# The first feed-forward product of a two-block layer by Strassen's seven products, and the last second product in token halves

## The chip, the core and the metric

The kernel runs on one core of one Trainium2 chip. The metric is device time in microseconds (us), the median of three runs. TensorE (PE in the views) multiplies, VectorE (DVE) and ScalarE (ACT) do the elementwise work, SyncE (SP) issues the loads and stores.

## The reference, cut to what matters

Two transformer blocks over 512 tokens of width 1024, in float32. The change is in the end of the second block:

```
def squared_relu_mlp(u, w_ff1, w_ff2):            # w_ff1 1024x4096, w_ff2 4096x1024
    hdn = jnp.square(jax.nn.relu(jnp.einsum('bld,df->blf', u, w_ff1)))
    return jnp.einsum('blf,fd->bld', hdn, w_ff2)
h = h + squared_relu_mlp(rmsnorm_2(h, norm_ffn[l]), w_ff1[l], w_ff2[l])
return rmsnorm_2(h, norm_final)[:, N_META:]
```

## The kernel before

Activations lie transposed: X is eight tiles of 128 features by 512 tokens. Each float32 operand of a product is split into a rounded part (`_hi`, made by ScalarE) and the rest (`_lo`, a subtraction on VectorE). `mm3` (lines 545 to 547) issues three matmuls for one product of tiles: hi by hi, lo of the activations by hi of the weights, hi by lo. Every matmul has its own weight load.

Weights come in units of 1 MB (1024 x 256 values, "a unit"). SyncE loads a unit into one of two `raw` buffers as soon as VectorE has split the unit before the last (`w_lo_ready`). ScalarE writes `w_hi` (L1372, L1792), VectorE `w_lo` (L1813), each 128x2048 in one instruction. A unit gives two output tiles of 128 x 512: 2 x 8 x 3 = 48 matmuls with 512 columns.

The stage before is the projection `w_out`: four units. VectorE adds each of its eight tiles to X (L2474), multiplies by the norm's gain into T (L2478) and, when ScalarE has made `C_hi`, writes `C_lo` (L1813). The norm's own factor is applied later: `norm_sums` (L574, L576) adds the squares over the features, ScalarE takes the root (L1388), VectorE the reciprocal (L1833) and its square, and the outputs of the second product are multiplied by it (L2507).

The feed-forward part, `hidden(it)`, goes through the 4096 hidden features in four groups (NFF = 4) of 1024. A group is four units of the first product (C by w_ff1; ScalarE takes relu into T, VectorE squares it, L2496, and both split it into `FF_hi`, `FF_lo`) and then four units of the second (FF by w_ff2; VectorE multiplies by the factor, L2507, and adds to X, L2510). TensorE's accumulators ("banks", 128 x 512, eight of them) are used in rotation of four. Each engine runs its own list of instructions in the order in which it is written; semaphores tie the lists. At the end a last norm: squares, sums over the features (L1347), root, reciprocal, transposes that spread it (L1353), eight multiplications (L2524) and eight stores.

Of the kernel before, what the change touches and what calls it, by code (L numbers as in the profile page):

```python
# [123 lines left out]
ZS = {_name: _i + 1 for _i, _name in enumerate(["k0", "k1", "k2", "k3", "lr0", "lr1", "q0", "q1"])}  # L124

# [15 lines left out]
def build(nc, t, out):  # L141
    with ExitStack() as ctx:
# [312 lines left out]
        relu_ready = sem("relu_ready")  # L455
# [19 lines left out]
        def full(h):  # L475
            return h[:, :] if len(h.shape) == 2 else h[:, :, :]

# [44 lines left out]
        def _(pe):  # L522
# [20 lines left out]
            def mm3(o, lhs, rhs, first, last):  # L543

                pe.matmul(o, lhs[0], rhs[0], start=first, stop=False)  # L545
                pe.matmul(o, lhs[0], rhs[1], start=False, stop=False)  # L546
                return pe.matmul(o, lhs[1], rhs[0], start=False, stop=last)  # L547
# [768 lines left out]
            def hidden(it):  # L1316
                u0 = U0["ffn"]
                FF = [FF_hi, FF_lo]
                for i in range(8):
                    pe.wait_ge(w_lo_ready, 8 * it + (u0 + i + 1))  # L1320
                    w = [dense(w_slot(u0 + i, h)) for h in (True, False)]
                    for j in range(2):
                        m = 2 * (i % 4) + j
                        o = tile((relu_ready, 8 * it + (m + 1)) if i < 4 else
                                 (x_ready, 8 * it + (X_BASE["ffn"] + KT + m + 1)))
                        for k in range(KT):
                            if it == 0 and i == 0 and j == 0:
                                pe.wait_ge(h_lo_ready, 24 + k + 1)
                            if i == 4 and j == 0:
                                pe.wait_ge(ff_lo_ready, 8 * it + (k + 1))  # L1330
                            ins = mm3(o[:, :], [x[:, k, j * P:(j + 1) * P] for x in w],
                                      [x[:, k, :] for x in ([C_hi, C_lo] if i < 4 else FF)], k == 0, k == KT - 1)
                        mark(ins, ("ff", it, i, j))
                        if it == 0 and i == 0 and j == 0:
                            norm_sums("ffn")

            for it in range(NFF):
                hidden(it)
# [25 lines left out]
        def _(act):  # L1364
# [403 lines left out]
            for i in range(4):  # L1768
                if i < 3:
                    split_hi(U0["w_out"] + i + 2)  # L1770
# [971 lines left out]
```

## Time and profile before

| | us |
|---|---|
| median of 3 runs (1920.85 to 1924.08) | 1923.98 |
| the profiled execution | 1926.47 |
| its span in the profile | 1924.7 |
| TensorE busy | 1872.8 (97%) |
| VectorE busy | 836.9 (43%) |
| ScalarE busy | 555.6 (29%) |

All times below are counted from the start of the span of the profiled execution. That a matmul is shown with 0.39 us does not mean that it takes that long from the next one: they are pipelined, and the pace is the distance of two starts.

### The profile page before, as it was taken

The page shows a single profiled execution, that of the slowest core. Times are in us where ns is not written, and L with a number is a line of the kernel's source. Part 1 is how long each engine was busy: PE and PEld are TensorE (multiplying, and loading weights), DVE is VectorE, ACT ScalarE, POOL GpSimd, SP SyncE. Part 2 cuts the span into 40 slices and gives each one's busy share as a digit, 9 for nine tenths or more (in the row PEclk, how much of TensorE's full clock was granted, in tenths as well). Part 3 has the DMA queues.
Part 4 walks back from the last instruction along what each step waited for, and adds up shares of the span by engine and source line. Part 5 has one row for each costly group of instructions (what it writes and reads, how often), then busy time and mean ns, then how long its engine had stood idle before and what let it go on. Part 6 is the DMA issues. An engine that isn't in the chain of part 4 may idle for free.

```text
span 1924.7 us, 20720 instructions
## 1 busy us (share of the span) xinstructions
PE 1872.8 (97%) x8962; PEld 1337.9 (70%) x8962; DVE 836.9 (43%) x1112; ACT 555.6 (29%) x737; POOL 0.2 (0%) x4
## 2 busy tenths in 40 slices
PE   7999999999999999999998998999999999999997
PEld 6788666688898785444443344997888778888886
DVE  6644345534563543011111013647665654444444
ACT  5322344433253321110100113444432332313131
POOL 0000000000000000000000000000000000000000
PEclk9999999999999999999999999899998999999999
DMA  5332211032243428999999997323221322232231
GB/s 183 94 104 88 75 41 36 23 113 88 88 154 118 166 74 360 427 428 428 427 428 428 427 428 271 86 89 88 66 66 59 95 88 88 88 110 88 90 99 53
DMA packets 135690, 324.68 MB, mean 169 GB/s; under 512 B 7328, under 2 KB 117168, under 8 KB 122288
## 3 DMA queue, kind: packets, MB, share of 16 engines
q1 hardware_dynamic: 135600, 323.36, 45.0%
q8 instruction: 71, 1.16, 0.2%
q14 instruction: 19, 0.16, 0.0%
HBM read 321.25 MB, written 2.10 MB: 168 GB/s over the span
## 4 chain that ended last, share of the span: by engine, by line
PE 86%; DMA 7%; DVE 4%; ACT 2%; issue 1%; SPq 0%; DVEq 0%; ACTq 0%
PE bank L545 19%; PE bank L547 19%; PE bank L546 19%; PE bank L1006 12%; DMA ew_f<-in_w_exp_up 3%; DMA ew_b<-in_w_exp_up 2%; PE bank L1028 2%; PE bank L976 2%; PE bank L737 1%; PE bank L713 1%; DMA ew_c<-in_w_exp_up 1%; ACT w_hi L1372 1%; DVE w_lo L1813 1%; PE bank L1197 1%; PE bank L717 1%
## 5 line engine op out<-in xcount | busy, mean ns | idle before, releaser
L1813 DVE TENSOR_TENSOR w_lo<-raw,w_hi 128x2048 fp32r<-128x2048 f32 x107 | 245.1, 2291 | 245.5 <-ACT w_hi L1372 220.1
L545 PE MATMUL bank<-H_hi,w_hi 128*128 128x512 f32 (+1 forms) x800 | 314.1, 393 | 3.0 <-DVE H_lo L1813 1.8
L546 PE MATMUL bank<-H_lo,w_hi 128*128 128x512 f32 (+1 forms) x800 | 308.8, 386 | 0.0
L547 PE MATMUL bank<-H_hi,w_lo 128*128 128x512 f32 (+1 forms) x800 | 308.7, 386 | 0.0
L1372 ACT ACTIVATE w_hi<-raw 128x2048 fp32r<-128x2048 f32 x77 | 146.9, 1908 | 149.4 <-PE bank L547 145.4
L545 PEld LDWEIGHTS bank<-H_hi,w_hi 128*128 128x128 f32 x800 | 150.0, 188 | 50.4 <-issue 14.4
L547 PEld LDWEIGHTS bank<-H_hi,w_lo 128*128 128x128 f32 x800 | 150.1, 188 | 33.4
L546 PEld LDWEIGHTS bank<-H_lo,w_hi 128*128 128x128 f32 x800 | 150.1, 188 | 32.5 <-issue 1.0
L545 PE MATMUL bank<-C_hi,w_hi 128*128 128x512 f32 x416 | 166.6, 401 | 5.4 <-DVE C_lo L1860 5.4
L546 PE MATMUL bank<-C_lo,w_hi 128*128 128x512 f32 x416 | 164.8, 396 | 0.0
L547 PE MATMUL bank<-C_hi,w_lo 128*128 128x512 f32 x416 | 164.8, 396 | 0.0
L2187 DVE SCALAR_TENSOR_TENSOR SG<-bank,gs,SG 128x512 f32<-128x512 f32 x16 | 11.3, 745 | 219.4 <-PE bank L1006 219.4
L545 PE MATMUL bank<-FF_hi,w_hi 128*128 128x512 f32 x256 | 101.1, 395 | 0.0
L546 PE MATMUL bank<-FF_lo,w_hi 128*128 128x512 f32 x256 | 101.1, 395 | 0.0
L547 PE MATMUL bank<-FF_hi,w_lo 128*128 128x512 f32 x256 | 101.1, 395 | 0.0
L545 PEld LDWEIGHTS bank<-C_hi,w_hi 128*128 128x128 f32 x416 | 78.4, 188 | 25.1 <-DVE w_lo L1813 5.5
L1792 ACT ACTIVATE w_hi<-raw 128x2048 fp32r<-128x2048 f32 x30 | 57.2, 1908 | 122.2 <-PE bank L547 122.2
L546 PEld LDWEIGHTS bank<-C_lo,w_hi 128*128 128x128 f32 x416 | 78.4, 189 | 19.7 <-issue 0.7
L547 PEld LDWEIGHTS bank<-C_hi,w_lo 128*128 128x128 f32 x416 | 78.3, 188 | 19.3
L1006 PE MATMUL bank<-ew_b,XG 128*64 128x512 f32 x256 | 80.7, 607 | 7.4 <-DMA ew_d<-in_w_exp_up 4.9
L1006 PE MATMUL bank<-ew_c,XG 128*64 128x512 f32 x224 | 80.2, 617 | 2.2 <-DMA ew_c<-in_w_exp_up 2.2
L1006 PE MATMUL bank<-ew_e,XG 128*64 128x512 f32 x128 | 57.9, 606 | 2.7 <-DMA ew_c<-in_w_exp_up 2.7
(403 smaller groups left out, 2925.9 us busy)
## 6 DMA issues: line engine op xcount, KB each, us to landing
raw<-in_w_in SPq DMA_DIRECT2D x38, 1024.0 KB, 5.5
raw<-in_w_ff SPq DMA_DIRECT2D x32, 1024.0 KB, 5.1
ew_b<-in_w_exp_up SPq DMA_DIRECT2D x9, 2048.0 KB, 25.5
ew_c<-in_w_exp_up SPq DMA_DIRECT2D x8, 2048.0 KB, 25.8
ew_b<-in_w_exp_gate SPq DMA_DIRECT2D x7, 2048.0 KB, 30.3
ew_c<-in_w_exp_gate SPq DMA_DIRECT2D x6, 2048.0 KB, 30.4
ew_c<-in_w_exp_down SPq DMA_DIRECT2D x6, 2048.0 KB, 25.7
ew_e<-in_w_exp_gate SPq DMA_DIRECT2D x5, 2048.0 KB, 31.6
```

The lines of the kernel that those rows point to most:

```text
L545: pe.matmul(o, lhs[0], rhs[0], start=first, stop=False)
L546: pe.matmul(o, lhs[0], rhs[1], start=False, stop=False)
L547: return pe.matmul(o, lhs[1], rhs[0], start=False, stop=last)
L713: pe.matmul(o[h][:, :], qn[:, h, c], kn[:, h, :], start=True, stop=False)
L717: mark(pe.matmul(o[h][:, :], qr[r, c], kr[r, :], start=False, stop=True), ("sc", t, h, i))
L737: ins = pe.matmul(bank[7][:, c:c + P], vt[:, h, j, :], pt[:, h, j, :], start=(j == 0), stop=(j == TT - 1))
L976: ins = pe.matmul(bank[4 + half][:, :], OH[:, tt, :], part[:, tt, half * S:(half + 1) * S], start=(tt == 0 and part is TK_hi), stop=(tt == ...
L1006: ins = pe.matmul(acc[half][r, :], lhs[:, k, r], views[e][:, j, half * S:(half + 1) * S], start=(k == 0), stop=(k == KT - 1))
L1028: ins = pe.matmul(o[:, :], part[:, m * P:(m + 1) * P], OT[:, p % 2, :], start=(part is YO_hi), stop=(part is YO_lo))
L1372: act.activation(w_slot(u, True), raw[:, u % RAW, :], ACT.Copy).then_inc(w_hi_ready, 1)
L1792: act.activation(w_slot(u, True), raw[:, u % RAW, :], ACT.Copy).then_inc(w_hi_ready, 1)
L1813: return dve.tensor_tensor(out=dst, in0=src, in1=hi_part.bitcast(F32), op=ALU.subtract)
```

## The change

The first product uses Strassen's scheme (in Winograd's form). A unit (256 hidden features) is a 2 by 2 arrangement of blocks: two output tiles of 128, by even and odd feature tiles; the activations are 2 by 2 as well: even and odd feature tiles by two halves of 256 tokens. Eight block products become seven. Each has 4 steps of `mm3`, so a unit has 7 x 4 x 3 = 84 matmuls of 256 columns. In exchange:

- of the activations three differences (`TR_sums`) are made per pair of tiles and split (`TR_hi`, `TR_lo`), once;
- of each unit's weights four sums or differences of blocks (`left_sums`, "s"), split beside the two blocks that are used as they are ("a") and a third ("d"): ScalarE 1024 + 512 + 2 x 1024 elements a row and VectorE 4 x 512 more than those;
- of the products, the running sum in one bank is copied by ScalarE after products 1, 6, 7 and 4 (`copied`), and TensorE waits for the copy before it adds to that bank; VectorE adds the other banks to these (`first_sums`, `middle_sums`, `last_sums`) and does relu and square in one instruction.

The units are put in another order (SEQ): the four first units of group 0, and from then on a unit of the first product of a group and a unit of the second product of the group before, in turn ("a round"). Group 3's second product comes last. It computes the first 256 tokens of all eight tiles, then the other 256, and the last norm and the stores are done by halves too.

```
+SEQ = [("one", 0, u) for u in range(4)]
+for _g in range(1, NFF):
+    for _u in range(4):
+        SEQ += [("one", _g, _u), ("two", _g - 1, _u)]
+SEQ += [("two", NFF - 1, _u) for _u in range(4)]
@@ TensorE
+            BANK = {1: 0, 2: 1, 5: 2, 3: 3, 6: 0, 7: 0, 4: 0}
+            def product(s, f, steps=range(4)):
+                o = product_banks(s)[BANK[f]]
+                for i in steps:
+                    ins = mm3(o[:, 0:HS], left(s, f, i), right(f, i), i == 0 and f in (1, 2, 5, 3), i == 3,
+                              skip_group_check=f in (6, 7, 4))
+            def first_unit():
+                pe.wait_ge(w_lo_ready, W_AT[j] + 3)
+                for i in range(3):
+                    for f, need in ((2, 1), (1, 2), (5, 2), (3, 2)):
+                        pe.wait_ge(h_lo_ready, 24 + 3 * i + need)
+                        product(s, f, (i,))
...
+                for f, copied in ((6, 1), (7, 2), (4, 3)):
+                    pe.wait_ge(part_copied, copied)
+                    product(s, f)
+                norm_sums("ffn")
+            def unit_one(g, u):
+                if s == 1:
+                    pe.wait_ge(std_ready, NORMS.index("ffn") + 1)
...
+                pe.wait_ge(w_lo_ready, W_AT[j] + 1)
+                product(s, 1)
+                product(s, 2)
+                pe.wait_ge(w_lo_ready, W_AT[j] + 2)
+                pe.wait_ge(part_copied, 4 * s + 1)
+                product(s, 6)
+                product(s, 5)
+                pe.wait_ge(w_lo_ready, W_AT[j] + 3)
+                pe.wait_ge(part_copied, 4 * s + 2)
+                product(s, 7)
+                product(s, 3)
+                pe.wait_ge(part_copied, 4 * s + 3)
+                product(s, 4)
+            def unit_two(g, u):
+                pe.wait_ge(w_lo_ready, W_AT[j] + 2)
...
+            for half in range(2):
+                for m in range(KT):
...
+                    if half == 1 and m == 2:
+                        final_sums(0)
+                    if half == 1 and m == 3:
+                        final_roots(0)
@@ ScalarE
+            for s in range(4 * NFF):
+                copied(s, 1)
+                if g:
+                    two_hi(g - 1, u)
+                else:
+                    left_parts(s + 1)
+                copied(s, 6)
+                copied(s, 7)
+                if s:
+                    hidden_hi(s - 1)
+                if g == 0:
+                    left_sums(s + 1)
+                copied(s, 4)
+                if s == 0:
+                    root("ffn")
+                if g and s + 1 < 4 * NFF:
+                    left_parts(s + 1)
+                    left_sums(s + 1)
@@ VectorE
+                x, d = squares_of(u), ring_of(s)["sums"]
+                link(dve.tensor_tensor(out=d[:, 0, :, :], in0=x["21"], in1=x["22"], op=ALU.add))
+                dve.tensor_tensor(out=d[:, 1, :, :], in0=d[:, 0, :, :], in1=x["11"], op=ALU.subtract)
+                dve.tensor_tensor(out=d[:, 2, :, :], in0=x["11"], in1=x["21"], op=ALU.subtract)
+                dve.tensor_tensor(out=d[:, 3, :, :], in0=x["12"], in1=d[:, 1, :, :], op=ALU.subtract)
...
+            for s in range(4 * NFF):
+                g, u = divmod(s, 4)
+                if s >= 5:
+                    second_out(*divmod(2 * (s - 4) - 1, 8))
+                first_sums(s)
+                if g == 0:
+                    left_sums(s + 1)
+                    left_lo(s + 1, 0)
+                else:
+                    two_lo(g - 1, u)
+                middle_sums(s)
+                if s:
+                    hidden_lo(s - 1)
+                if g == 0:
+                    left_lo(s + 1, 1)
+                    left_lo(s + 1, 2)
+                last_sums(s)
+                if s == 3:
+                    norm_start("ffn")
...
+                if g:
+                    second_out(*divmod(2 * (s - 4), 8))
```

VectorE's list at the end of `w_out` and the start of the feed-forward part, before (TR_, ring_ and p_ do not exist):

```order
L2474 TENSOR_TENSOR X<-bank,X 128x512
L2478 TENSOR_SCALAR T<-X,vecs 128x512
L1827 TENSOR_TENSOR sq<-sq 128x512
L1813 TENSOR_TENSOR C_lo<-T,C_hi 128x512 x2
L1813 TENSOR_TENSOR w_lo_52<-raw,w_hi_51 128x2048
L1833 RECIPROCAL rstd<-std 128x512
```

The same place after it, from the weights of the first unit (ring_first) over the last two tiles of X to the first addition of products:

```order
L2059 TENSOR_TENSOR ring_first_a_lo<-raw,ring_first_a_hi 128x1024
L2059 TENSOR_TENSOR ring_first_d_lo<-raw,ring_first_d_hi 128x512
L2059 TENSOR_TENSOR ring_first_s_lo<-ring_first_sums,ring_first_s_hi 128x1024 x2
L2750 TENSOR_TENSOR X<-bank,X 128x512
L2757 TENSOR_SCALAR T<-X,vecs 128x512
L2750 TENSOR_TENSOR X<-bank,X 128x512
L2754 TENSOR_SCALAR T<-X,vecs 128x512
L2759 TENSOR_TENSOR TR_sums<-T 128x256
L2760 TENSOR_TENSOR T<-T 128x256
L2763 TENSOR_TENSOR TR_sums<-T 128x256
L2764 TENSOR_TENSOR TR_sums<-T,TR_sums 128x256
L2073 TENSOR_TENSOR sq<-sq 128x512
```

The four differences and the split of the first unit's weights now stand between the last tiles of X and the C_lo that the first products read.

VectorE's list after the change from the third unit's last part to the split of the first unit of w_ff2 (w_lo_52; `TS` and `T` hold hidden tiles of odd and even units):

```order
L2797 TENSOR_TENSOR TS<-bank,TS 128x256
L2801 SCALAR_TENSOR_TENSOR TS<-TS 128x512 x2
L2079 RECIPROCAL rstd<-std 128x512
L2843 TENSOR_TENSOR rstd<-rstd 128x512
L2784 TENSOR_TENSOR T<-bank,p_195 128x256
L2059 TENSOR_TENSOR w_lo_52<-raw,w_hi_51 128x1024 x2
L2790 TENSOR_TENSOR T<-bank,p_196 128x256
L2792 TENSOR_TENSOR T<-bank,p_197 128x256
L2059 TENSOR_TENSOR FF_lo<-TS,FF_hi 128x512 x2
```

The reciprocal of the norm, which stood ahead of all hidden tiles, now stands after the fourth unit's hidden tiles and ahead of the weights for the second product.

## Rows read from the trace of the kernel before

**Rows 1.** The page: span, and busy time by engine (us, share, instructions).
```profile
span 1924.7 us, 20720 instructions
PE 1872.8 (97%) x8962; PEld 1337.9 (70%) x8962; DVE 836.9 (43%) x1112; ACT 555.6 (29%) x737; POOL 0.2 (0%) x4
```
**Rows 2.** Busy time by stretch: w_out, feed-forward in three pieces, what follows.
```profile
core 0: us, PE busy (x) PEld busy (x) DVE busy (x) ACT busy (x) POOL busy (x), PEclk, DMA share, GB/s
1516.98:1551.78 34.80, 34.80 (x150) 27.92 (x149) 21.64 (x28) 12.63 (x16) 0.00 (x0) 1.00 0.39 121
1551.78:1596.58 44.80, 44.80 (x190) 35.40 (x189) 25.02 (x24) 17.13 (x21) 0.00 (x0) 1.00 0.27 85
...
1866.88:1911.89 45.01, 45.01 (x194) 36.15 (x193) 22.42 (x26) 11.37 (x13) 0.00 (x0) 1.00 0.07 24
1911.89:1924.70 12.81, 2.65 (x21) 2.24 (x19) 6.92 (x11) 0.89 (x2) 0.00 (x0) 0.70 0.44 164
```
**Rows 3.** Waits, 1551.78 to 1911.89: who for whom, us, times, longest.
```profile
ACT w_hi L1792 <- PE bank L547: 122.2, 14, 9.3
...
DVE ffo L2507 <- PE bank L547: 74.9, 26, 4.2
```
**Rows 4.** Timeline (start, us, instruction), first tile of the feed-forward part.
```profile
1552.02 0.39 PE L546 MATMUL bank<-C_lo,w_hi 128*128 128x512 f32 x1
...
1557.15 0.39 PE L547 MATMUL bank<-C_hi,w_lo 128*128 128x512 f32 x1
1557.38 1.02 PE L574 MATMUL bank<-sq,ones 128*128 128x512 f32 x2
```
**Rows 5.** Timeline, the product with the memory keys (256 columns), first block.
```profile
535.54 0.28 PE L545 MATMUL bank<-MM_hi,w_hi 128*128 128x256 f32 x1
...
541.72 0.28 PE L547 MATMUL bank<-MM_hi,w_lo 128*128 128x256 f32 x1
```
**Rows 6.** Tile MM_hi: weight loads, ns minimum/median/maximum.
```profile
L545 PEld LDWEIGHTS bank<-MM_hi,w_hi x64: 186/187/189, 535.3 to 559.2; 128*128 128x128 f32 x64
```
**Rows 7.** Groups by line and shape, VectorE (busy us, mean ns of one).
```profile
L2339 DVE TENSOR_TENSOR F<-B 128x1024 f32<-128x1024 f32 x6 | 7.3, 1211 | 0.0
L1813 DVE TENSOR_TENSOR MM_lo<-memx,MM_hi 128x256 fp32r<-128x256 f32 x8 | 3.0, 418 | 0.0
```
**Rows 8.** The same for ScalarE.
```profile
L1715 ACT ACTIVATE F<-F 128x1024 f32<-128x1024 f32 x6 | 6.4, 1061 | 35.7 <-DVE F L2342 35.7
L1543 ACT ACTIVATE mk<-bank 128x256 f32<-128x256 f32 x8 | 2.9, 371 | 1.7 <-PE bank L547 1.7
```
**Rows 9.** Timeline, VectorE and ScalarE around the norm.
```profile
1535.20 1.29 DVE L1813 TENSOR_TENSOR C_lo<-T,C_hi 128x512 fp32r<-128x512 f32 x2
1536.40 0.68 DVE L2474 TENSOR_TENSOR X<-bank,X 128x512 f32<-128x512 f32 x1
...
1551.98 0.69 DVE L2474 TENSOR_TENSOR X<-bank,X 128x512 f32<-128x512 f32 x1 [3.10 <-PE bank L547]
...
1559.30 0.69 ACT L1388 ACTIVATE std<-bank,vecs 128x512 f32<-128x512 f32 x1 [3.05 <-PE bank L576]
...
1560.02 3.35 DVE L1833 RECIPROCAL rstd<-std 128x512 f32<-128x512 f32 x1 [1.44 <-ACT std L1388]
```
**Rows 10.** The page: loads of w_ff units (KB, us from issue to landing).
```profile
raw<-in_w_ff SPq DMA_DIRECT2D x32, 1024.0 KB, 5.1
```
**Rows 11.** Busy time by stretch, after small matmuls of the gated attention.
```profile
1470.00:1474.00 4.00, 4.00 (x13) 3.19 (x13) 0.75 (x1) 0.60 (x1) 0.00 (x0) 0.59 0.00 0
```
**Rows 12.** Timeline, the end.
```profile
1911.66 0.39 PE L547 MATMUL bank<-FF_hi,w_lo 128*128 128x512 f32 x1
...
1914.29 1.05 PE L1347 MATMUL bank<-ones,sq 128*128 128x1 f32 x8 [1.45 <-ACT sq L1384]
...
1915.97 0.65 PE L1353 MATMUL bank<-ident,rstd_t 128*128 128x128 f32 x4 [0.64 <-DVE rstd_t L2521]
1916.66 5.36 DVE L2524 SCALAR_TENSOR_TENSOR X<-X,vecs,bank 128x512 f32<-128x512 f32 x8 [0.74 <-PE bank L1353]
```

More of the change, by code:

```diff
@@ L541, in flush, with mm3 @@
                         pending[b] = None
[L543 to L547, printed above, removed]
+            def mm3(o, lhs, rhs, first, last, **kw):
+                pe.matmul(o, lhs[0], rhs[0], start=first, stop=False, **kw)
+                pe.matmul(o, lhs[0], rhs[1], start=False, stop=False, **kw)
+                return pe.matmul(o, lhs[1], rhs[0], start=False, stop=last, **kw)
             def unit(u, kt=8):
@@ L1337, in _ @@
-            for it in range(NFF):
-                hidden(it)
-            n = NORMS.index("fin2")
-            pe.wait_ge(std_ready, n)
-            for j in range(2):
-                if j:
-                    pe.wait_ge(sq_ready, 8 * n + KT)
-                else:
-                    pe.wait_ge(acc_ready, ACC_AT["fin2"] + 6)
-                for tt in range(TT):
-                    ins = pe.matmul(bank[4][:, tt:tt + 1], sq[:, j, tt * P:(tt + 1) * P], ones[:, 0:1],
-                                    start=(j == 0 and tt == 0), stop=(j == 1 and tt == TT - 1))
@@ new lines, in _, with final_sums @@
+            flush()
+            first_unit()
+            for kind, g, u in SEQ[1:-4]:
+                if kind == "one":
+                    unit_one(g, u)
+                else:
+                    unit_two(g, u)
+            pe.wait_ge(ff_ready, 8 * NFF)
+            n_tile[0] = 0
+            n = NORMS.index("fin2")
+            def final_sums(half):
+                pe.wait_ge(std_ready, n + half)
+                for j in range(2):
+                    if j:
+                        pe.wait_ge(sq_ready, 8 * n + KT * half + KT)
+                    else:
+                        pe.wait_ge(acc_ready, ACC_AT["fin2"] + 6 * half + 6)
+                    for tt in (2 * half, 2 * half + 1):
+                        ins = pe.matmul(bank[4][:, tt:tt + 1], sq[:, j, tt * P:(tt + 1) * P], ones[:, 0:1],
+                                        start=(j == 0 and tt == 2 * half), stop=(j == 1 and tt == 2 * half + 1))
+                marks.tile = bank[4]
+                mark(ins, ("fin_ss", half))
@@ new lines, in last_sums @@
+            def last_sums(s):
+                h = hidden_of(s)
+                o = done(dve, ("p", s, 3))
+                link(dve.tensor_tensor(out=h[:, 0, HS:S], in0=o[:, 0:HS], in1=h[:, 0, HS:S], op=ALU.add))
+                for j in range(2):
+                    if j:
+                        dve.wait_ge(part_copied, 4 * s + 4)
+                    dve.scalar_tensor_tensor(out=h[:, j, :], in0=h[:, j, :], scalar=0.0, in1=h[:, j, :],
+                                             op0=ALU.max, op1=ALU.mult).then_inc(ff_ready, 1)
```

440 lines of the change are left out of this document (326 added, 114 removed).

## The prediction

> **What bounds the kernel now.** I read the page first, then the busy time by stretch, then the waits, then the timeline. TensorE is busy for 1872.8 of 1924.7 us, VectorE for 43% [rows 1]. In the feed-forward part, 1551.78 to 1911.89, TensorE is busy for the whole of each stretch at a granted clock of 1.00, and VectorE for about half of it [rows 2]; the waits there are those of VectorE and ScalarE for TensorE [rows 3]. The stretch of 360.1 us is 32 units of 48 matmuls and a norm sum. In the first tile 22 steps take 5.13 us, 0.2333 us each [rows 4]: a unit takes 11.2 us, 32 take 358.4, and the norm sum has 1.7 (two times 0.86, by the starts from 1557.38). So nothing is lost there, and only fewer or quicker matmuls can shorten it. From 1911.89 to 1924.7 a chain of small steps runs with TensorE nearly idle [rows 2, 12].
>
> **1. Matmuls, -22.4 us.** Whether 84 matmuls of 256 columns are cheaper than 48 of 512 hangs on the pace at 256 columns. The product with the memory keys has just this shape, the same three-fold form and a weight load for each: 53 steps in 6.18 us, 0.1166 us each [rows 5], half of 0.2333, although a weight load lasts 0.187 us [rows 6]. So a unit takes 84 x 0.1167 = 9.8 us, and 16 units save 16 x 1.4 = 22.4. The last group's halves, 384 matmuls in place of 192, cost 0 at this pace.
>
> The rows show that weight loads overlap the matmuls: the load's 0.187 us is longer than the pace. The Trainium skill, "TensorE: Matmul & The Clock Gate", section "The mechanism", speaks against the change: a weight load overlaps matmuls in flight only if its row group differs, and here all are 128 by 128. By the page's own times (an estimate: 0.107 us for a load, as much for 256 columns and 0.213 for 512) a unit would go from 48 x 0.32 = 15.4 to 84 x 0.213 = 17.9 us. The trace doesn't agree, neither at 512 columns (0.2333) nor at 256 (0.1167).
>
> **2. The first unit, +5.4 us.** Durations, from rows: VectorE 0.69 us for 512 elements a row, 1.21 for 1024, 0.42 for 256, each 0.08 less when the next follows without depending on it (two C_lo in 1.29, the next start 1.20 after the first) [rows 7, 9]; ScalarE 1.06 for 1024 and 0.37 for 256 out of a bank [rows 8]; from a tile's end to the next engine 0.20 us (1551.78 to 1551.98) [rows 9], and about 0.05 back to TensorE. In w_out VectorE is busy 21.6 of 34.8 us [rows 2]. It gets, for each pair of tiles, four differences (1.75) and a split of 768 elements (0.87), and for the first unit 2.55 (four sums) and 4.03 (their split, 1.14 + 0.6 + 2 x 1.14), and loses two splits of 2.2. I laid its list out from the start of w_out: the last w_out tiles end when they did (1551.78), because the w_lo that they need are done at 1523.7 and 1534.9, long before 1529.4 and 1540.6. But the differences are at the latest place: tile 4 of X is added at 1541.0, the first unit's weights are ready at 1552.8, X 6 and 7 at 1553.5 and 1554.8, the last C_lo at 1558.3 and 1558.9, TR_lo at 1559.8. TensorE starts at 1552.9 (1.1 late), does three of four steps of products 2, 1, 5, 3 (4.2 us, to 1557.1), waits for C_lo (1.5) and ends these at 1560.0. Products 6, 7 and 4 follow one another in one bank, and between them stands only the copy: 0.20 + 0.37 + 0.07 = 0.65 us, twice exposed (1.3). Then the norm sum, 1.7 as before, and now a wait for the root, which unit 1's banks need: 0.20 + 0.69 + 0.05 = 0.95 [rows 9]. Sum 1.1 + 1.5 + 1.3 + 0.95 = 4.9, and five restarts at 0.1. Bounds: 2.3 if VectorE keeps up, 9 if each new instruction there takes a quarter more.
>
> **3. The first group's rounds, +3.0 us.** Here no second product lies between, so a round of TensorE is 9.8 us. VectorE has in it 0.34 + 2.55 + 1.75 + 0.8 + 1.2 + 2.3 + 1.8 = 10.7, and with a wait for ScalarE about 10.9: it slips by 1.1 a round. This stays hidden at first. From the start of unit s, the addition after product 2 comes at 3.0 and the first part of the next unit's weights is ready at 7.6; with slips of 1.1 and 2.1 at 8.7 and 9.7, still under 9.8 (0.2 for the second part of unit 4). But after unit 3 VectorE has the reciprocal (3.35) and its square (0.69) [rows 9], and only then product 2 of unit 4 (0.34) and the weights of the second product (2.3). They are ready 22.5 us after unit 3's start, TensorE is there at 19.6 + 0.2: it waits 2.8. Queued behind is the split of the last hidden tiles, 24.5, needed after six steps at 26.7. Bounds: 0 if VectorE's instructions overlap better, 8 if it is a quarter slower (three rounds of 2 us more).
>
> In the 12 rounds of groups 1 to 3 TensorE has 9.8 + 11.2 = 21.0 us, VectorE 15.5. From a round's start: addition 3.4, second product's weights 5.8 (needed at 9.8), hidden tiles 9.5, relu and square 11.3 (after product 4's copy), sums 13.8, next weights 15.6, 16.7, 17.9 (needed at 21.0, 23.8, 26.6), output 19.3. ScalarE copies at 1.6, 4.4, 7.2 and 10.0; the two halves of w_hi (1.0 each) end at 4.0, before the second copy is due; SyncE's load goes out 15 us before it is used and takes 5.1 [rows 10]. So each copy is back before the product after next. This I cost at 0: its cover is 4 us at least, at each of the three places where VectorE is waited for.
>
> **4. The last group, +1.4 us.** Its weights: units 0 and 1 are split before the second product of group 2 is out, units 2 and 3 when their loads have landed (25.7 and 28.0 after the last round's start, split by 29.0 and 31.3, needed at 32.2 and 37.8). VectorE comes to the first output tile at 31.3 and frees its bank at 32.2, with TensorE there at the same time: 0.2. The first half's norm sum and transposes now stand among the matmuls: eight small matmuls in about 1.0 us, and two transposes of four that take 0.65 [rows 12]: 1.2. Bounds: 0.4 to 2.5.
>
> **5. The end, -3.3 us.** Before: 12.8 us from the last matmul's end (1911.66 + 0.23). After, on 256 columns: output and addition 0.27 less each, square 0.23 less, norm sum 0.45 less, transposes 0.25 less, the eight multiplications at 0.40 in place of 0.67 (8 in 5.36 [rows 12]) 2.1 less; the last store as long as before. That is 3.5; I take off 0.2 for the stores, whose issues now follow every 0.4 us. Bounds: -4.2 and -2.
>
> **Sum.** -22.4 + 5.4 + 3.0 + 1.4 - 3.3 = -15.9 us. From the profiled execution's 1926.5 that gives 1910.6; the median shown is 2.5 lower, so I forecast 1908.
>
> **Rivals.**
> A: VectorE keeps up better than I laid out, because I let it wait at each link. Terms 2 and 3 fall to 2.3 and 0, the sum to -22: 1902. For it: pairs of instructions overlap by 0.08 [rows 9]. Against: the differences depend on each other, and the reciprocal can't be hidden.
> B: VectorE bounds the first group, if strided blocks of 128 or the fused relu and square are a quarter dearer than plain 512. Term 2 becomes 9 and term 3 8: sum -7.3, 1916.7. For it: it is the one place without slack, with 10.7 of 9.8 us. Against: its time here goes by elements (256, 1024 and 512 lie on one line, 1.04 ns each and 0.15 [rows 7, 9]).
> C: the clock. At 1470 to 1474, behind a stretch of small matmuls, the granted clock was 0.59 on average, mostly at the lower of its levels, 1.2 GHz [rows 11]. The first unit has gaps of 0.65 to 1.5 us in 16 us. If it sets in there and lasts for 3 to 10 us, it costs half of that: 1910 to 1913.
> D, the other side: the pace at 256 columns. 1728 matmuls are issued at it, so the gain of 15.9 is gone when it is 0.1167 + 15.9/1728 = 0.1259 us, 8% above what [rows 5] show, and at a floor of the weight load's 0.187 [rows 6] the kernel is slower by 1728 x 0.070 - 15.9 = 105, 2029 us. For it: that product ran while ScalarE and VectorE had less to do, and its matmuls stayed in a bank for a whole tile, where here a product ends every 12. Against: the pace did not move within 53 steps, and at 512 columns it is the same 560 cycles of 2.4 GHz with all engines at work. The page's rule above would give an end on this side too.
> E: the change fails to do what it says, because a copy comes late in every steady round. It would have to cost 15.9/12 = 1.3 us a round; ScalarE would have to be late by 0.8 + 1.3. Nothing in its layout is.
>
> **How the numbers follow.** Forecast 0.64, A 0.10, B 0.12, C 0.08, D 0.03, E 0.03. What the measurement can tell from no change is 0.2%, 3.9 us. All but D and E stay beyond it, with part of E within: faster 0.94, same 0.02, slower 0.04. The range from 1901 to 1916 holds the forecast, A, C and half of B.
>
> **What would show it.** Right: 128x256 matmuls start 0.117 apart; in the steady rounds TensorE has no wait and two units take 21.0; one wait of about 3 us for VectorE ahead of the first unit of w_ff2, and five short ones in the first unit; the last matmul ends near 1898 to 1900, with 9.5 us behind it. Wrong: a wait for `part_copied` in each round, a granted clock under 1.00 after 1556, or a pace above 0.12.

## The result: 1904.4 us, and the profile after

The changed kernel took 1904.4 us (median of 4 runs, 1903.5 to 1909.4), the kernel before beside it 1924.0 (4 runs, 1920.9 to 1925.9): a ratio of 0.9911, 95% interval 0.9886 to 0.9935. A second set of runs (after2, below) gave 0.9914, 0.9899 to 0.9928. The profiled execution took 1904.18 us, its span 1902.4.

The page of the changed kernel, which answers to [rows 1]:

```profile
span 1902.4 us, 22765 instructions
PE 1844.8 (97%) x9730; PEld 1355.7 (71%) x9730; DVE 940.8 (49%) x1355; ACT 592.1 (31%) x846; POOL 0.2 (0%) x4
```

TensorE has 768 more matmuls and is busy 28 us less; VectorE is busy 104 us more. Busy time by stretch, as in [rows 2]: w_out, the gap before the first unit, the first unit with its norm sum and the root, one steady round, and what follows the last matmul.

```profile
core 0: us, PE busy (x) PEld busy (x) DVE busy (x) ACT busy (x) POOL busy (x), PEclk, DMA share, GB/s
1508.14:1542.94 34.80, 34.80 (x150) 27.79 (x149) 31.49 (x48) 16.10 (x21) 0.00 (x0) 1.00 0.31 93
1542.94:1545.73 2.79, 0.17 (x2) 0.04 (x1) 2.68 (x5) 0.64 (x2) 0.00 (x0) 1.00 0.95 271
1545.73:1561.43 15.70, 13.98 (x88) 12.22 (x88) 13.17 (x22) 8.09 (x13) 0.00 (x0) 0.89 0.19 57
1698.38:1719.38 21.00, 21.00 (x134) 18.81 (x133) 15.66 (x22) 8.06 (x12) 0.00 (x0) 1.00 0.32 101
1893.23:1902.40 9.17, 1.34 (x9) 0.93 (x8) 4.23 (x11) 0.68 (x2) 0.00 (x0) 0.72 0.36 120
```

w_out takes the same 34.80 us, but ends at 1542.94 where it ended at 1551.78. From there to the span's end it is 359.46 us in place of 372.92. So only 13.5 of the 22.3 us between the two profiled executions lie in the stretch that the change touches; 8.8 lie ahead of it.

The timeline at the first unit, VectorE and TensorE (start, us, instruction, idle time before it and what ended it):

```profile
1541.42 2.36 DVE L2059 TENSOR_TENSOR ring_first_s_lo<-ring_first_sums,ring_first_s_hi 128x1024 fp32r<-128x1024 f32 x2
1543.69 0.69 DVE L2750 TENSOR_TENSOR X<-bank,X 128x512 f32<-128x512 f32 x1
1544.93 0.69 DVE L2750 TENSOR_TENSOR X<-bank,X 128x512 f32<-128x512 f32 x1
1545.73 0.52 PE L614 MATMUL bank<-C_hi,ring_first_a_hi 128*128 128x256 f32 x1 [2.62 <-DVE X L2750]
...
1548.50 1.29 DVE L2059 TENSOR_TENSOR C_lo<-T,C_hi 128x512 fp32r<-128x512 f32 x2
...
1555.11 0.38 PE L614 MATMUL bank<-TR_hi,ring_first_s_hi 128*128 128x256 f32 x1 [0.47 <-ACT p L1989]
...
1561.43 0.39 PE L614 MATMUL bank<-C_hi,ring_odd_a_hi 128*128 128x256 f32 x1 [0.78 <-ACT std L1560]
```

The weights of the first unit are done at 1543.78, but TensorE waits for tile 7 of X, until 1545.73. C_lo, done at 1549.79, is no longer waited for. Unit 1 starts 18.49 us after the end of w_out; without any loss it would be 9.8 us of products and 1.7 of norm sum, 11.5. The granted clock in the first 16 matmuls was half, that is 1.2 GHz; the busy time by stretch says it:

```profile
1545.73:1549.11 3.38, 3.38 (x16) 3.38 (x17) 3.24 (x8) 2.62 (x4) 0.00 (x0) 0.51 0.19 68
```

The timeline ahead of the first unit of w_ff2, which answers to the reciprocal in [rows 9]:

```profile
1596.33 3.35 DVE L2079 RECIPROCAL rstd<-std 128x512 f32<-128x512 f32 x1
1599.71 0.69 DVE L2843 TENSOR_TENSOR rstd<-rstd 128x512 f32<-128x512 f32 x1
...
1600.78 2.35 DVE L2059 TENSOR_TENSOR w_lo<-raw,w_hi 128x1024 fp32r<-128x1024 f32 x2
...
1603.18 0.50 PE L614 MATMUL bank<-FF_hi,w_hi 128*128 128x512 f32 x1 [1.74 <-DVE w_lo L2059]
```

And the last group and the end, as in [rows 12]:

```profile
1853.53 2.02 ACT L2010 ACTIVATE w_hi<-raw 128x1024 fp32r<-128x1024 f32 x2 [1.11 <-DMA raw<-in_w_ff]
...
1857.93 0.36 PE L614 MATMUL bank<-H_hi,w_hi 128*128 128x256 f32 x1 [1.08 <-DVE X L2891]
...
1893.23 0.42 DVE L2888 TENSOR_TENSOR ffo<-bank,rstd 128x256 f32<-128x256 f32 x1 [0.87 <-PE bank L616]
...
1894.67 0.61 PE L1494 MATMUL bank<-ones,sq 128*128 128x1 f32 x4 [1.14 <-ACT sq L2041]
...
1895.90 0.43 PE L1505 MATMUL bank<-ident,rstd_t 128*128 128x128 f32 x2 [0.62 <-DVE rstd_t L2871]
1896.37 3.22 DVE L2878 SCALAR_TENSOR_TENSOR X<-X,vecs,bank 128x256 f32<-128x256 f32 x8 [0.53 <-PE bank L1505]
```

From 1603.18 to the last group's start at 1845.49 TensorE has no wait at all: 242.3 us, which is one unit of w_ff2 (11.2) and eleven rounds of 21.0.

### The profile page after: what moved, and what is told of

Same layout as the page of the kernel before. It is cut to its first block, busy times and chain, and to the rows that moved or that the text cites. A ratio compares the mean times of both kernels' runs of the same rounds, so it can differ in the third digit from the quotient of the medians.

```text
span 1902.4 us, 22765 instructions
## 1 busy us (share of the span) xinstructions
PE 1844.8 (97%) x9730; PEld 1355.7 (71%) x9730; DVE 940.8 (49%) x1355; ACT 592.1 (31%) x846; POOL 0.2 (0%) x4
## 3 DMA queue, kind: packets, MB, share of 16 engines
q8 instruction: 77, 1.26, 0.3%
## 4 chain that ended last, share of the span: by engine, by line
PE 82%; DVE 7%; DMA 7%; ACT 2%; issue 1%; SPq 0%; DVEq 0%; ACTq 0%
PE bank L614 18%; PE bank L616 17%; PE bank L615 17%; PE bank L1075 12%; DMA ew_f<-in_w_exp_up 3%; DMA ew_b<-in_w_exp_up 2%; DVE w_lo L2059 2%; PE bank L1097 2%; PE bank L1045 2%; PE bank L806 2%; PE bank L782 1%; DMA ew_c<-in_w_exp_up 1%; ACT w_hi L1544 1%; PE bank L1266 1%; PE bank L786 1%
## 5 line engine op out<-in xcount | busy, mean ns | idle before, releaser
L614 PE MATMUL bank<-H_hi,w_hi 128*128 128x512 f32 (+2 forms) x992 | 376.0, 379 | 4.1 <-DVE H_lo L2059 1.8
L615 PE MATMUL bank<-H_lo,w_hi 128*128 128x512 f32 (+2 forms) x992 | 370.5, 373 | 0.0
L616 PE MATMUL bank<-H_hi,w_lo 128*128 128x512 f32 (+2 forms) x992 | 370.4, 373 | 0.0
L2059 DVE TENSOR_TENSOR w_lo<-raw,w_hi 128x2048 fp32r<-128x2048 f32 (+1 forms) x107 | 209.3, 1970 | 221.2 <-ACT w_hi L1544 217.5
L1544 ACT ACTIVATE w_hi<-raw 128x2048 fp32r<-128x2048 f32 x75 | 143.0, 1907 | 138.7 <-PE bank L616 134.8
L614 PE MATMUL bank<-C_hi,w_hi 128*128 128x512 f32 x160 | 65.3, 408 | 5.3 <-DVE C_lo L2106 5.3
L1075 PE MATMUL bank<-raw,XG 128*64 128x512 f32 x128 | 58.0, 608 | 6.7 <-DMA ew_f<-in_w_exp_up 6.7
L615 PE MATMUL bank<-C_lo,w_hi 128*128 128x512 f32 x160 | 64.0, 400 | 0.0
L616 PE MATMUL bank<-C_hi,w_lo 128*128 128x512 f32 x160 | 64.0, 400 | 0.0
L1075 PE MATMUL bank<-ew_f,XG 128*64 128x512 f32 x128 | 58.1, 609 | 1.0 <-DMA ew_a<-in_w_exp_up 1.0
```

The costliest lines, as they stand in the source:

```text
L614: pe.matmul(o, lhs[0], rhs[0], start=first, stop=False, **kw)
L615: pe.matmul(o, lhs[0], rhs[1], start=False, stop=False, **kw)
L616: return pe.matmul(o, lhs[1], rhs[0], start=False, stop=last, **kw)
L1075: ins = pe.matmul(acc[half][r, :], lhs[:, k, r], views[e][:, j, half * S:(half + 1) * S], start=(k == 0), stop=(k == KT - 1))
L1544: act.activation(w_slot(u, True), raw[:, u % RAW, :], ACT.Copy).then_inc(w_hi_ready, 1)
L2059: return dve.tensor_tensor(out=dst, in0=src, in1=hi_part.bitcast(F32), op=ALU.subtract)
```

## The experiments

The theories. N: the reciprocal of the norm on VectorE makes the wait at 1603. F: the wait for the last banks of w_out makes the late start of the first unit. C: the clock falls there because TensorE has stood idle. P: VectorE's added work in the steady rounds is hidden, up to the limit that the forecast's layout gives. L: that w_out ended 8.8 us earlier is chance and not the change. "Rest" is the time from the end of w_out to the end of the span.

**The kernel before, a second profiled execution (before2).** Nothing is edited.

> The kernel before, unchanged, once more. In the two profiled executions (1924.7 before, 1902.4 after) the last w_out tile ended at 1551.8 and at 1542.9, though nothing ahead of w_out was changed. Theory L (chance): the 8.9 us are where the granted clock fell, 0.92 against 0.94 in 1190 to 1280 and 0.65 against 1.00 in 1460 to 1470; then this execution ends w_out somewhere between 1542 and 1552, and its span from there on is 372.9 us, within 0.3, as before. Theory S (systematic: the changed kernel is laid out otherwise in memory and its unchanged part runs faster): this one ends w_out at 1551 to 1552 again, and each variant of the changed kernel near 1543.

Measured: 1925.46 us, w_out ends at 1549.51, rest 374.19. It ends 2.3 us from where the first execution had it, with 1.3 us more behind it, which is outside the 0.3 that was expected. The 1.3 us lie behind the last matmul: 14.08 us at a mean granted clock of 0.57, where [rows 2] have 12.81 at 0.70. Two executions do not settle L; the section behind the experiments has all of them.

**The reciprocal later (e_norm).**

```diff
-                if s == 3:
+                if s == 4:
                     norm_start("ffn")
```

> The changed kernel with the reciprocal of the feed-forward norm and its square moved on VectorE by one round, behind the hidden tiles of unit 4. Theory N: the 1.9 us that TensorE waits ahead of the first unit of w_ff2 are these two instructions (4.1 us) in VectorE's way; moved, the weights are split 4.1 us earlier and the wait is 0, from the end of w_out to the end of the span 359.5 becomes 357.5, and nothing is late afterwards, since the next round had 1.4 us of idle VectorE and 5.6 us of cover. Rival D: VectorE is full through the whole first group, so the 4.1 us come back as a wait in the next round, sum 359.5.

Measured: 1907.95 us, rest 358.10, 1.4 less than the changed kernel. The reciprocal now stands behind the w_lo that were late, and the unit of w_ff2 starts without a wait:

```profile
1601.75 2.35 DVE L2059 TENSOR_TENSOR w_lo<-raw,w_hi 128x1024 fp32r<-128x1024 f32 x2
1607.68 3.35 DVE L2079 RECIPROCAL rstd<-std 128x512 f32<-128x512 f32 x1
...
1618.33 0.68 DVE L2820 TENSOR_TENSOR ffo<-bank,rstd 128x512 f32<-128x512 f32 x1
```

Its result, squared by 1611.8, is first read at 1618.33, so it had 6.6 us to spare. N holds, and the forecast's remark under rival A that the reciprocal can't be hidden does not: one round later it is. In the last group, which this edit does not touch, the wait for a bank was 1.61 us where the changed kernel's was 1.24 (1.08 idle, and the restart); so the 1.9 us did not come back in full.

**Waiting for each bank by itself (e_bank).**

```diff
                     for f, need in ((2, 1), (1, 2), (5, 2), (3, 2)):
+                        if pending[BANK[f]] is not None:
+                            pe.wait_ge(*pending[BANK[f]])
+                            pending[BANK[f]] = None
                         pe.wait_ge(h_lo_ready, 24 + 3 * i + need)
...
-            flush()
             first_unit()
```

> The changed kernel, but TensorE starts the first unit's products without waiting for all four banks of w_out: each product waits only for its own bank. Theory F: the start at 2.8 us after w_out (forecast 1.1) is late because the list waits there for tile 7's addition to X, which VectorE does 1.9 us after the first unit's weights; now products 2 and 1 start 0.9 to 1.0 us after w_out and product 3 waits for tile 7, and the first C_lo of the last pair becomes the later wait. The first unit ends 1.0 to 2.0 us earlier. Theory C: the granted clock fell to half at the start (16 matmuls 0.213 us apart instead of 0.117, 1.6 us) because of that 2.8 us gap; with a gap of 1.0 it stays at 1.00 and another 1.6 us go, part of it hidden by the wait for C_lo. Rival W: the weights of the first unit are the late part, then the start does not move.

Measured: 1909.91 us, rest 360.57. The start did not move: 2.77 us after w_out, and the half-clock stretch behind it cost 1.63 us as before. The reason stands in the program's order with buffer numbers: w_out's tiles run through four banks, tile 7 lies in bank 1, and the first product that is issued, product 2, writes bank 1. So the edit asked first for the very bank that comes free last. This experiment did not test F; e_first does.

**VectorE with 3.8 us more in each steady round (e_dve3).** Three copies of the split of the a squares are added from unit 5 on (units are counted from 0).

```diff
                     x = squares_of(U0["ffn"] + j)
+                    for _ in range(3 if s > 4 else 0):
+                        link(rest(r["a"][1][:, :, :, :], x["a"], r["a"][0][:, :, :, :]))
```

> The changed kernel with three more VectorE subtractions of 128x1024 (they repeat one that is there, and write the same values) in each round from unit 5 on: 11 x 3 x 1.26 = 42 us more of VectorE's work. Theory P: a steady round is bound by TensorE, 21.0 us, and VectorE has 15.5 us of work and 1.6 us of waits in it, so 3.8 us more are hidden: change 0 to +1 us in all. Rival V: VectorE's list is as long as the round for its waits, and each round becomes longer: +11 x 1 us or more.

Measured: 1912.16 us, rest 361.01. All of TensorE's waits from 1600 to 1856:

```profile
PE bank L614 <- DVE w_lo L2059: 1.7, 1, 1.7
PE bank L614 <- DVE ring_even_d_lo L2059: 0.3, 1, 0.3
```

The first is the one at w_ff2; the second stands in the round behind it (0.50 us with the restart). VectorE is busy 979.2 us in place of 940.8: 38 us of added work, 3.5 in each of eleven rounds, cost TensorE half a microsecond of waiting. The rest is 1.55 us more than the changed kernel's, above the 0 to 1 that was expected. Beside that half it holds 0.2 in the last group and 0.5 in which no wait stands: every second steady round takes 21.09 us in place of 21.00, and it does so in e_bank and e_whole too, which have no added work. P holds up to here.

**The changed kernel once more, timed in five rounds (after2).** Nothing is edited.

> The changed kernel, unchanged, for a closer ratio to before and as the measure of the next two. Theory L (chance ahead of w_out): its gain over before is near the 13.5 us that the stretch from w_out to the end lost (372.9 to 359.5), ratio 0.993. Theory S (the unchanged part is faster too): 17 to 22 us, ratio 0.989 to 0.991.

Measured: 1908.73 us (1905.87 to 1910.32), the kernel before 1925.64 (11 runs), ratio 0.9914, 0.9899 to 0.9928. The gain is 16.9 us by the medians, between the 13.5 that theory L gave and the 17 to 22 of its rival, and next to the rival. Rest 362.46, 3.0 more than in the first execution. The difference lies in the last group: the wait for the bank was 2.48 us here (1.24 in the first), and behind it stood a second stretch at 1.2 GHz:

```profile
1858.56:1861.96 3.40, 3.40 (x19) 3.40 (x17) 2.67 (x7) 1.25 (x3) 0.00 (x0) 0.50 0.00 0
```

So the term of the last group differs between these two executions by 3 us.

**Four edits together (e_best).** e_norm and e_bank; the norm's sums go to bank 7, so that unit 1 asks for the root only ahead of product 3; the last weights of w_ff2 are split behind the first two output tiles of the last group.

```diff
+            return bank[7] if name == "ffn" else bank[4]
...
                 product(s, 7)
+                if s == 1:
+                    pe.wait_ge(std_ready, NORMS.index("ffn") + 1)
                 product(s, 3)
...
-            two_lo(NFF - 1, 3)
...
+                    if half == 0 and m == 1:
+                        two_lo(NFF - 1, 3)
```

> The changed kernel with four waits of TensorE taken away: the norm's reciprocal behind unit 4's hidden tiles (1.9 us), a wait for each bank instead of for all in the first unit (1 to 2 us, and 1.6 if the clock stays up), the norm sum in bank 7 with the wait for its root ahead of unit 1's product 3 (1.0), and the last unit's w_lo behind the first two output tiles (1.2). Expected: 5 to 7 us less than the changed kernel from the end of w_out on, 359.5 to about 353.5. Rival: VectorE is the bound of the first group, so that what the first unit gains comes back as waits for the weights of units 2 to 4: 2 to 3 us less only.

Measured: 1906.44 us (1904.15 to 1911.35), ratio 0.9904, 0.9887 to 0.9921. Rest 355.41, 4.1 less than the changed kernel's 359.46. The wait for the root, the one at w_ff2 and the one in the last group are gone; the late start (2.77) and its half-clock stretch (1.56) are still there, which is why the gain stays under the 5 to 7 us that were expected with them. By whole times it can't be told from the changed kernel, since the executions of both spread over 4 to 7 us; in the traces, the waits that it takes away are gone.

**The last group in whole tiles (e_whole).** The second product of the last group as in the kernel before, 192 matmuls of 512 columns with one norm sum and one set of stores; all else as changed.

```diff
-            for half in range(2):
-                c = token_half(half)
                 for m in range(KT):
```

> The changed kernel, but the last group's second product and the last norm with all 512 tokens at once, as before. By the traces the token halves cost 1.2 us for the sums and transposes among the matmuls, 1.2 for a late bank and 0.2 of restarts, and take 3.4 us off the end (12.8 to 9.4). Theory H: without them the stretch from the end of w_out is 0.6 to 1.0 us longer, 360.3. Rival: the halves also keep VectorE from the work in time, and without them it is shorter.

Measured: 1910.31 us (1904.70 to 1913.07), ratio 0.9920, 0.9903 to 0.9937; rest 360.87, 1.4 more than the first execution of the changed kernel and 1.6 less than the second (expected: 0.6 to 1.0 more). So the halves are worth 1.4 us at the most by these, and their sign is not shown. What they give at the end is seen in the timeline of e_whole's end:

```profile
1891.12 0.40 PE L616 MATMUL bank<-H_hi,w_lo 128*128 128x512 f32 x1
...
1896.59 5.36 DVE L2845 SCALAR_TENSOR_TENSOR X<-X,vecs,bank 128x512 f32<-128x512 f32 x8 [1.21 <-PE bank L1508]
```

The last matmul, started at 1891.12, ends 13.3 us before the span's end, against 9.4 us with halves. Most of this 3.9 us is paid for ahead of it.

**VectorE with 7.6 us more in each steady round (e_dve6).** As e_dve3, with six copies.

> The changed kernel with six more VectorE subtractions of 128x1024 in each round from unit 5 on, 7.6 us a round. Theory P: this is more than VectorE's spare time (21.0 less 15.5 of work leaves 5.5, less 1.6 if all waits stay), so now VectorE is the bound: a round of 23.2 to 24.5 us, +18 to +33 us in all, with TensorE waiting for w_lo in each. Rival V': TensorE has buffers enough to hide it: under +10 us.

Measured: 1947.03 us, rest 396.54, 37 more than the changed kernel. TensorE's waits from 1600 to 1860:

```profile
PE bank L614 <- DVE ring_even_d_lo L2059: 22.0, 10, 4.1
PE bank L614 <- DVE w_lo L2059: 1.7, 1, 1.7
```

The waits, with their restarts, are 4.28 us once and then about 2.15 in each round (the last of these ten stands behind 1860); a round takes 23.2 us where the clock stays up. Here P has its limit: TensorE's 21.0 us leave VectorE 21.0 - 15.7 = 5.3 us of room in a round; 3.5 more is hidden, twice that is not. The whole is above the 18 to 33 us that were expected, because stretches at 1.2 GHz stood behind the waits: 6.8 us with 29 matmuls behind the first, which cost 2.9 us, and 3.4 us behind five of the other ten, 1.5 us each.

**The banks in another order (e_first).**

```diff
+            if s == 0:
+                return [bank[3], bank[2], bank[0], bank[1]]
             return bank[4:8] if odd(s) else bank[0:4]
...
-                pe.wait_ge(w_lo_ready, W_AT[j] + 3)
-                for i in range(3):
-                    for f, need in ((2, 1), (1, 2), (5, 2), (3, 2)):
+                for part, fs in ((1, ((2, 1), (1, 2))), (3, ((5, 2), (3, 2)))):
+                    pe.wait_ge(w_lo_ready, W_AT[j] + part)
+                    for f, need in fs:
...
+                        for i in range(3):
```

> The first unit's products take their four banks in another order: the product that is issued first writes the bank of the attention output projection's tile 4, the next that of tile 5, the last that of tile 7 (in the changed kernel the first product writes the bank of tile 7, so waiting for each bank by itself had moved nothing), three steps of each product run before the next, and the first two wait only for the plain weight squares. Theory F (the bank of tile 7 and the order are what holds the start): the first product starts within 0.3 us of the end of w_out in place of 2.77 us after it, and the wait moves to C_lo of tile 7, ready 6.2 to 6.9 us after w_out's end; the unit ends 1.5 to 2.5 us earlier. Theory C (the granted clock falls because of the gap at the start): the 16 matmuls at 0.213 us are gone from there if no gap of 2.8 us is left; another 1.6 us. If instead the change of shape (128x256 matmuls after 128x512) makes the clock fall, the half-clock stretch stands at the same place without a gap. From the end of w_out to the span's end: 355 to 357 us where changed kernel has 359.5 to 362.5, by theory F and C; 357.5 to 359 by F alone; 360 to 362 if something else holds the start.

The lines left out wait for the product's own bank. Measured: 1902.47 us (one run), rest 357.80. TensorE's timeline around the end of w_out:

```profile
1542.67 0.39 PE L618 MATMUL bank<-H_hi,w_lo 128*128 128x512 f32 x1
1542.90 0.28 PE L616 MATMUL bank<-C_hi,ring_first_a_hi 128*128 128x256 f32 x1
...
1549.18 0.39 PE L616 MATMUL bank<-C_hi,ring_first_a_hi 128*128 128x256 f32 x1 [1.90 <-DVE C_lo L2065]
```

The first product follows 0.23 us behind w_out's last matmul, with nothing between. From 1542.90 to unit 1 at 1559.41 it is 16.51 us in place of 18.49, and the granted clock over it:

```profile
1542.90:1559.41 16.51, 12.88 (x89) 10.74 (x88) 15.83 (x26) 8.75 (x14) 0.00 (x0) 1.00 0.34 98
```

The mean is 1.00, and the stretch of half-clock matmuls is gone, though the shape changes from 512 to 256 columns at the same place. F and C hold as causes: the gap and the slow stretch are gone. But their sizes do not add up, because TensorE now comes to C_lo of tile 7 earlier and waits 2.06 us for it, the wait that the forecast had. Unit 1 starts 1.98 us earlier, where F by itself had 1.5 to 2.5 and C another 1.6. So the rest is 0.8 us above the range for F and C together and in the one for F alone, though the trace shows both. With a start at once, the 1.6 us would have been hidden by the wait for C_lo (an estimate from the 2.06); it was wrong to add them.

**The best version (e_best2).** The edits of e_best (with e_first's order in place of e_bank's), and VectorE's list at the first unit changed: the split of the d square and the last accumulation for the norm, 1.2 us together, stand behind C_lo and TR_lo of tiles 6 and 7, and the load that reuses the buffer of the d square waits for it.

```diff
-                accumulate("ffn", [m for m in (2 * i, 2 * i + 1) if 1 <= m < KT - 1])
+                if i < 3:
+                    accumulate("ffn", [m for m in (2 * i, 2 * i + 1) if 1 <= m < KT - 1])
...
+                if i == 3:
+                    rest(r["d"][1][:, :, :], ...["22"], r["d"][0][:, :, :]).then_inc(w_lo_ready, 1)
+                    accumulate("ffn", [m for m in (2 * i, 2 * i + 1) if 1 <= m < KT - 1])
```

> The version of e_best (norm's reciprocal behind unit 4, root awaited later and its sums in bank 7, last second-product weights split behind the first halves), with e_first's bank order, and VectorE doing the d square's remainder of the first unit and the last norm accumulation behind C_lo and TR_lo of tiles 6 and 7 instead of ahead of them. C_lo of tiles 6 and 7 should be ready 5.0 and 5.7 us after w_out's end, so the wait ahead of the fourth step is 0.8 to 1.2 us where e_first has about 2. From w_out's end to the span's end: 351 to 353 us if the clock stays up in the first unit, 353 to 355 if it falls once (e_best: 355.4). In whole time 2 to 4 us below e_best's 1906.4, that is 1902 to 1905, ratio to the kernel before 0.988 to 0.990.

Measured: 1896.08 us (1895.45 to 1901.33), the kernel before 1922.36 (9 runs), ratio 0.9875, 0.9853 to 0.9896. This is below both kernels: its interval does not touch that of after2, though it overlaps the wider one of the first four runs. Rest 351.94, as expected. The timeline at the first unit:

```profile
1543.10 0.68 DVE L2768 TENSOR_TENSOR X<-bank,X 128x512 f32<-128x512 f32 x1
...
1547.30 1.29 DVE L2072 TENSOR_TENSOR C_lo<-T,C_hi 128x512 fp32r<-128x512 f32 x2
1548.04 0.39 PE L619 MATMUL bank<-C_hi,ring_first_a_hi 128*128 128x256 f32 x1 [0.70 <-DVE C_lo L2072]
```

Counted from the end of w_out, C_lo comes 1.2 us earlier than in e_first, and TensorE is idle for 0.70 us in place of 1.90. The whole time came out below the 1902 to 1905 that were expected. That sum started from e_best's median on another chip, 1906.44; less the 1.8 us outside the span and the rest of 355.4, w_out ended there at about 1549 (an estimate), and here it ended at 1542.96.

**The kernel before, a third profiled execution (before3).** Nothing is edited.

> The kernel before once more. Theory L (where w_out ends is chance, unchanged code): w_out ends anywhere between 1541 and 1555 us, and from there to the end 372.9 to 374.2 us as in the two executions seen. If the changed kernel's text made the unchanged part faster, w_out would end at 1549.5 or later again.

Measured: 1925.30 us, w_out ends at 1550.62, rest 372.88. This lies in what theory L allowed and also in what its rival did (1549.5 or later), so it does not decide between them.

## Where w_out ends, over thirteen executions

The stages ahead of w_out are the same code in all, and w_out itself takes 34.80 us before and after; what is seen to differ is the granted clock on the way. From 1460 to 1480, the place of [rows 11], first the kernel before (before2), then e_best, then the changed kernel:

```profile
1460.00:1480.00 20.00, 20.00 (x102) 17.75 (x103) 6.89 (x12) 3.24 (x7) 0.00 (x0) 0.74 0.00 0
```

```profile
1460.00:1480.00 20.00, 20.00 (x110) 18.13 (x109) 4.87 (x9) 2.64 (x6) 0.00 (x0) 0.74 0.16 53
```

```profile
1460.00:1480.00 20.00, 20.00 (x115) 17.14 (x115) 11.66 (x17) 5.80 (x9) 0.00 (x0) 1.00 0.00 1
```

A mean of 0.74 over 20 us is 5 us of clock lost. The dip stands in all three executions of the kernel before and in three of the ten of versions of the changed one (e_dve3, e_best, e_dve6). These six end w_out at 1550.7 on average, the seven without it at 1544.2 (1541.6 to 1548.0). So the changed kernel's text does not remove the dip, and the 8.8 us of the first pair are mostly this. But three of three against three of ten is not the same share either, and the averages over all executions, 1550.6 and 1546.2, differ by 4.4 us. This fits what the ratio leaves over: a ratio of 0.9914 is 16.6 us less than 1925.6, of which the rests (373.3, mean of three, less 361.0, mean of two) explain 12.4.

The traces say more. Ahead of w_out's end, TensorE stood at 1.2 GHz for 47.8, 44.4 and 44.4 us in the kernel before, and for 20.5 to 47.8 us in the ten others. Take half of that time off, which is what it costs, and w_out ends at 1527.3 to 1528.4 before and at 1527.2 to 1531.4 after. So the unchanged part is not quicker in anything but the granted clock. Nor is the kernel before bound to the slower clock: three of its nine timed executions beside e_first and e_best2 had spans of 1914.6 to 1917.0 us, which less the rest of 373.3 puts w_out's end at 1541 to 1544 (an estimate; these have no trace). Whether the 4 us on average are chance or follow from something that the change shifts ahead of w_out, no run settles.

## Why the forecast came out as it did

The profiled execution, by the forecast's own steps, from w_out's end on:

| step | forecast, us | measured, us |
|---|---|---|
| 1 matmuls | -22.4 | -21.75 |
| 2 first unit | +5.4 | +7.0 |
| 3 first group's rounds | +3.0 | +2.0 |
| 4 last group | +1.4 | +2.7 |
| 5 the end | -3.3 | -3.4 |
| sum | -15.9 | -13.5 |
| ahead of w_out's end | 0 | -8.8 |

**The mechanism was right in its main lines.** The change gains by matmuls and pays at the first unit, at the first unit of w_ff2 and a little in the last group; the measured median, 1904.4, lies in the range, 3.6 us under the forecast. Of the signs named beforehand, the pace (but for units 1 and 3), the steady rounds and the time behind the last matmul came as said; the one long wait was 1.9 us and not about 3, the first unit had one gap of 2.8 and three short waits in place of five short ones, and one of the signs of being wrong, a granted clock under 1.00 in the first unit, was there too.

**Step 1** held. The pace at 256 columns is 0.1167 us in a steady unit (9.80 us for 84), with VectorE and ScalarE at work beside it, which was the doubt of rival D. Units 1 and 3 alone are slower, 10.16 and 10.07 us with no wait to show for it; they are the two that read ring_odd and write banks 4 to 7. By the Trainium skill, "TensorE: Matmul & The Clock Gate", section "The mechanism", a weight load overlaps matmuls in flight only where its row group differs, or, as the same section has it, where it goes to the background weight buffer. The trace does not agree with the first: all loads here are 128 by 128, last 0.188 us, and go with matmuls that start 0.1167 us apart. Which buffer they went to, no run shows.

**Step 2** was mis-sized, in two terms. "TensorE starts at 1552.9 (1.1 late)" was worked out from the weights of the first unit, and these were in time, 0.84 us behind w_out. What failed is that TensorE, before the first unit, waits for every bank of w_out to be read, tile 7 of X included; that tile was in the forecast's own list of VectorE, 2 us behind the weights, and was not set against the first product. The start was 2.79 us late. e_first, which starts at once, shows this term. The second is rival C, put at 0.08 and as an alternative to the forecast: the clock did fall, for 16 matmuls, 1.6 us. Its cause was the late start, and not the short gaps inside the unit that the rival named. It fell in each of the eight executions with the 2.8 us gap and in neither of the two without it. Against these, the wait for C_lo (1.5) did not come, because the late start had covered it; in e_first, with no late start, it was 2.06 with the restart. Copies (1.3) and root (0.95) were as forecast: 1.26 and 0.94. So the forecast's 5.4 came nearer to the measured 7.0 than its parts did, by luck: 3.3 us too little in two of them, 1.5 too much in the third.

**Step 3**: the place and the cause were right (e_norm), the size was 1.9 us with 0.1 behind it, not 2.8 and 0.2. VectorE slipped less in the first rounds than laid out, the nearest to rival A that was seen.

**Step 4** was too small. "With TensorE there at the same time: 0.2" was 1.24 in the profiled execution and up to 2.5 in another, since the last weights were ready later than laid out: the last w_lo was done at 1856.98, 32.5 us after the last round's start where the forecast had 31.3, and the output tile that frees the bank stood behind it. Splitting these weights later (e_best) takes the wait away. The sums and transposes cost the 1.2 us that were forecast.

**Step 5** was right: 9.4 us behind the last matmul, 9.5 forecast.

**The steady rounds**, costed at 0, held: 21.00 us, VectorE busy 15.66 (15.5 forecast). e_dve3 and e_dve6 show the cover that was claimed: between 3.5 and 7 us a round. Rival B is ruled out in the steady rounds by this, and in the first group by its 1.9 us; rival E because TensorE has no wait for a copy from 1603 to 1845.

So the changed stretch gained 2.4 us less than the forecast's sum, and the time came out lower than the forecast because of the stretch ahead of it. That the forecast is near the median is partly luck: had w_out ended where it did before, the time would have come out 2.4 us above the forecast (13.5 gained for 15.9), or 3.5 by the averages of the rests.

## What to carry to other kernels

When a new stage takes over banks (or any buffers) from the stage before, put its first writes on those that come free first, and look at which tile each holds: here that, the root awaited later and three pieces of VectorE's work put behind what TensorE waits for gave 7.5 us more (rest 351.94 against 359.46, one profiled execution each). A gap on TensorE can cost more than its length: price it with the stretch at the lower clock that may follow. And compare stretches, from a landmark common to both traces, before a difference of whole times is explained.

## What the runs showed of the hardware

- Behind an idle stretch of 2.8 us at the first unit the granted clock was 0.51 for 3.4 us (16 matmuls at 0.213 us), in eight of eight executions, though in two of them (e_dve3, e_best) it fell only 1.0 and 0.7 us after the restart; without the gap, in two of two, it stayed at 1.00, and the wait of 2.06 us for C_lo in e_first did not bring it down. Behind the wait of 2.48 us in the last group it fell in after2, behind waits of 1.24 to 1.77 us there (after, e_norm, e_bank, e_dve3, e_first) it did not. In e_dve6 it fell behind the wait of 4.28 us and behind five of the ten waits of 2.15 us.
- The pace of equal matmuls depends on something that no wait shows: 0.120 us in the units that read ring_odd, their weight loads too, where it is 0.1167 with ring_even. The summary of one tile, minimum, median and maximum in ns, of ring_odd and then of ring_even:

```profile
L614 PEld LDWEIGHTS bank<-TR_hi,ring_odd_s_hi x16: 191/192/193, 1564.3 to 1588.1; 128*128 128x128 f32 x16
L614 PE MATMUL bank<-TR_hi,ring_odd_s_hi x16: 283/284/284, 1564.4 to 1588.2; 128*128 128x256 f32 x16
```

```profile
L614 PEld LDWEIGHTS bank<-TR_hi,ring_even_s_hi x104: 186/188/190, 1574.3 to 1831.0; 128*128 128x128 f32 x104
L614 PE MATMUL bank<-TR_hi,ring_even_s_hi x104: 277/279/282, 1574.4 to 1831.1; 128*128 128x256 f32 x104
```

  The two differ in the weights' place and in the banks written (4 to 7 against 0 to 3); which of these it is was not tried. It may be neither: in e_bank, e_dve3 and e_whole every second steady round took 21.09 us in place of 21.00, with ring_even and banks 0 to 3 in all of them and no wait.
